# Buffers shifted to multiples of 128 bytes, the first norm's squares added on VectorE, and a mixer projection that waits for emptied banks and has a third pair of weight tiles

## The reference

```python
def hybrid_layer(x, ...):                        # first layer, T = 512, D = 1024
    h = rmsnorm(x, g_mix)                        # x * rsqrt(mean(x*x)) * g
    z = h @ w_in                                 # 7 parts of 1024 features
    rnn_x, rnn_y, conv_b, conv_c, conv_x, gate_rnn, gate_conv = split(z)
    rnn_x = causal_depthwise_conv(rnn_x, conv4_w) + conv4_b
    y_rnn = gelu(rnn_y) * rg_lru(rnn_x, ..., lru_lambda)   # 4 heads; a scan over the tokens
    y_conv = conv_b * causal_depthwise_conv(conv_c * conv_x, conv3_w)
    merged = sigmoid(gate_rnn) * y_rnn + sigmoid(gate_conv) * y_conv
    x = x + merged @ w_out                       # the mixer projection
    g, u = split(rmsnorm(x, g_ffn) @ w_gate_up)
    x = x + (silu(g) * u) @ w_down               # 2816 wide
    return x + sigmoid(rmsnorm(x, g_ple) @ w_ple_gate) * (p @ w_ple)
# second layer: projections, sparse and latent attention, an output projection, then
#   a layer of 16384 experts: every token's product with all expert rows u (gelu),
#   top 16 of 8 heads chosen by product keys, weighted sum of the expert rows v
```

## The kernel before

| Tile | Role | Bytes past a multiple of 128 |
|---|---|---|
| `spl` | stationary | 64 |
| `w3` | stationary | 96 |
| `hh`, `hl`, `hu`, `lu`, `mixh`, `mixl`, `wsp` | moving | 96 |
| `acth`, `actl` | moving | 32 |

## Time and profile before

### The profile page before, as it was taken

One profiled execution on the slowest core, in us unless ns is written; L12 is line 12 of the kernel. 1 busy time (PEld: TensorE's weight loads), 2 busy tenths in 40 slices (PEclk: granted clock), 3 DMA queues, 4 the chain that ended last, 5 costly groups with the idle time before them and its releaser, 6 DMA issues.

```text
span 2835.9 us, 37050 instructions
## 1 busy us (share of the span) xinstructions
PE 2731.8 (96%) x13240; PEld 2244.3 (79%) x13240; DVE 1830.4 (65%) x2459; ACT 907.9 (32%) x1531; POOL 1691.3 (60%) x755
## 2 busy tenths in 40 slices
PE   7999989999998999998999999999999999999999
PEld 6777768878775776445888888888898999999998
DVE  5999963262225434665539983999963677777776
ACT  2223212101122234664234443444432333333332
POOL 5888867777764621002745455777776565665564
PEclk9999989999998998999999999999999999999999
DMA  3343324323322322001334546888898666766664
GB/s 141 132 133 129 126 101 137 129 95 130 121 93 72 104 81 103 1 1 47 117 106 139 146 143 181 258 279 282 282 319 310 231 259 238 265 244 254 256 241 159
DMA packets 171119, 466.66 MB, mean 165 GB/s; under 512 B 12832, under 2 KB 86688, under 8 KB 171040
## 3 DMA queue, kind: packets, MB, share of 16 engines
q1 hardware_dynamic: 152608, 398.53, 42.1%
q0 software_dynamic: 18432, 67.12, 6.6%
HBM read 404.78 MB, written 60.82 MB: 164 GB/s over the span
## 4 chain that ended last, share of the span: by engine, by line
PE 83%; issue 7%; DVE 4%; POOL 4%; ACT 1%; DMA 0%; POOLq 0%; SPq 0%; DVEq 0%; ACTq 0%
PE ps L1013 37%; PE ps L547 32%; POOL spl L2074 3%; PE ps L948 2%; PE ps L1034 2%; PE ps L925 1%; PE ps L908 1%; PE ps L641 1%; PE ps L563 1%; PE ps L904 1%; PE ps L569 1%; PE ps L867 1%; PE ps L736 1%; PE ps L701 0%; PE ps L813 0%
## 5 line engine op out<-in xcount | busy, mean ns | idle before, releaser
L2074 POOL TENSOR_TENSOR spl<-ring,spl 128x1024 fp32r<-128x1024 f32 x256 | 660.4, 2580 | 513.7 <-ACT spl L1367 513.6
L2016 POOL TENSOR_TENSOR spl<-ring,zero 128x1024 fp32r<-128x1024 f32 (+2 forms) x181 | 365.4, 2019 | 561.5 <-PE ps L547 499.6
L547 PE MATMUL ps<-hh,spl 128*128 128x512 f32 x2064 | 664.8, 401 | 17.7 <-DVE hl L1493 7.3
L1013 PE MATMUL ps<-wsp,spl 128*128 128x448 f32 x3072 | 638.6, 370 | 4.6 <-issue 4.6
L1013 PEld LDWEIGHTS ps<-wsp,spl 128*128 128x128 f32 x3072 | 578.7, 189 | 62.2 <-POOL spl L2074 5.0
L1013 PE MATMUL ps<-hh,spl 128*128 128x448 f32 x2048 | 606.6, 372 | 5.8 <-POOL spl L2074 5.8
L1367 ACT ACTIVATE spl<-ring 128x1024 fp32r<-128x1024 f32 x256 | 271.7, 1061 | 817.2 <-PE ps L1013 815.5
L2018 POOL TENSOR_TENSOR spl<-ring,spl 128x1024 fp32r<-128x1024 f32 (+2 forms) x181 | 481.3, 2659 | 14.2
L547 PEld LDWEIGHTS ps<-hh,spl 128*128 128x128 f32 x2064 | 391.0, 189 | 124.5 <-issue 14.0
L1974 DVE TENSOR_TENSOR wsp<-gl,wsp 128x448 fp32r<-128x448 f32 x128 | 310.6, 2427 | 184.1 <-ACT wsp L1412 183.9
L1013 PEld LDWEIGHTS ps<-hh,spl 128*128 128x128 f32 x2048 | 385.2, 188 | 46.5 <-issue 8.6
(11 more groups left out here) (338 smaller groups left out, 3348.2 us busy)
## 6 DMA issues: line engine op xcount, KB each, us to landing
ring<-stream_in SPq DMA_DIRECT2D x196, 704.0 KB, 4.1
ring<-u_in SPq DMA_DIRECT2D x128, 512.0 KB, 4.1
ring<-v_in SPq DMA_DIRECT2D x128, 512.0 KB, 3.5
gelu<-gst SPq DMA_DIRECT2D x128, 224.0 KB, 4.2
dense<-stage SPq DMA_DIRECT2D x14, 2048.0 KB, 13.5
gl<-gelu SPq DMA_DIRECT2D x32, 896.0 KB, 5.8
gw<-dense SPq DMA_DIRECT2D x32, 896.0 KB, 8.5
x<-x_in SPq DMA_DIRECT2D x4, 512.0 KB, 6.2
```

The source lines that it names most:

```text
L547: m = pe.matmul(ps[:, bank, :], w[:, part, k0 + k * n:k0 + k * n + P], rhs(k), start=first and k == 0 and part == 0 and rhs is high, stop= ...
L1013: m = pe.matmul(ps[:, bank, 0:TD], w[:, part, k0 + k * P:k0 + (k + 1) * P], rhs(k), start=first and k == 0 and part == 0 and rhs is high, ...
L2016: pool.tensor_tensor(w[:, 0, 0:n], ring[:, j, 0:n], zero[:, :].to_broadcast([P, n]), ALU.add).then_inc(wt_high, 1)
L2074: pool.tensor_tensor(spl[:, j % 2, 1, 0:D], ring[:, j, 0:D], spl[:, j % 2, 0, 0:D].bitcast(F32), ALU.subtract).then_inc(lo_done, 1)
```

## The change

1. Pads (`lead`, `mid`, `gap`) and another order of the buffers put every operand named in the table above at a multiple of 128 bytes, `w3` and the new `w4` too, and with them most other operands of matmuls (`identb`, `mqk`, `qk`, `xc`, `hnt`, `blk`, `pr`, `pt`). `cst`, with the ones and the identity, stays 64 bytes past one.
2. The first norm is done like the others: ACT squares chunk 0 into PSUM bank 7 and the rest into `sq1`, DVE adds them (7 additions), PE sums the result once (4 matmuls, 8 instructions). DVE does this and the scaling of the norm ahead of most of the softplus steps, which now stand behind them; ACT waits for them (`sp_ready`) at the first tanh.
3. The units 0 to 3 of the mixer projection wait until ACT has emptied their bank (`z_evac`) in place of `x_add`. The third unit has a tile pair of its own, `w4`, which lies where head 3 had `xc` and `r_g`; POOL splits it when the seventh chunk is merged (`chunk_done`), whatever PE has finished.

```diff
@@ buffers
+        rn = sb("rn", [P, 2, TT])
+        sb("lead", [P, 8])
...
-        rn = sb("rn", [P, 2, TT])
...
+        sp = sb("sp", [P, 6, DC], c=mix)
         mix.close()
...
-        sp = sb("sp", [P, 6, DC], c=one)
         rg = ExitStack()
-        rxp = sb("rxp", [P, 2, 3 + T], c=rg)
-        prod = sb("prod", [P, 2, 2 + T], c=rg)
+        mixh = [sb("mixh0", [P, DC // 2, T], F32R, c=rg), mixh1]
         zb = {n: sb(f"z_{n}", [P, 2, T], c=rg) for n in ("ry", "cb", "cc", "cx", "gr", "gc")}
+        fourth = ExitStack()
+        w4 = sb("w4", [P, 2, D], F32R, c=fourth)
+        fourth.close()
...
+        rxp = sb("rxp", [P, 2, 3 + T], c=rg)
+        prod = sb("prod", [P, 2, 2 + T], c=rg)
+        sb("mid", [P, 16], c=rg)
...
-        mixh = [mixh1, sb("mixh0", [P, DC // 2, T], F32R, c=rg)][::-1]
...
+        sb("gap", [P, 24], c=two)
@@ PE
             def mixed(c, k0, k1, ready=None):
                 if k0 == 0:
-                    pe.wait_ge(x_add, X_BASE[U_OUT] + c + 1)
+                    if c < 4:
+                        pe.wait_ge(z_evac, HEADS_RG * 14 + c + 4)
+                    else:
+                        pe.wait_ge(x_add, X_BASE[U_OUT] + c + 1)
                     pe.wait_ge(wt_low, U_OUT + c + 1)
-                return split_products(3 + c % 4, spl[:, c % 2, :, :], ...
+                return split_products(3 + c % 4, w4[:, :, :] if c == 2 else spl[:, c % 2, :, :], ...
...
-            for c in range(DC):
-                pe.wait_ge(col_sq, c + 1)
-                column(sq1[:, c % SQ_RING, :], c == 0, c == DC - 1)
+            added_column(0)
             row(0)
@@ ACT
-                if c >= SQ_RING:
-                    eng.wait_ge(col_used, c - SQ_RING + 1)
-                eng.activation(sq1[:, c % SQ_RING, :], x[:, c, :], ACT.Square).then_inc(col_sq, 1)
+                square_of(0, c)
...
-            eng.wait_ge(sp_ready, 2)
...
+                        if first:
+                            eng.wait_ge(sp_ready, 2)
@@ DVE
+            dve.sem_inc(x_add, 4)
...
+            for c in range(1, DC):
+                add_square(0, c)
+            column_inverse(0)
+            scale_parts(0, "g_mix")
             dve.wait_ge(sp_exp, 1)
...
-            column_inverse(0)
-            scale_parts(0, "g_mix")
...
-            dve.sem_inc(x_add, 4)
             for k in range(DC - 2, DC):
                 mix_part(k, k + 1)
@@ POOL
-                    pool.wait_ge(col_used, DC)
+                    pool.wait_ge(col_used, 1)
...
-            with pool.Fori(1, U_DOWN // RING) as i:
+            with pool.Fori(1, U_OUT // RING) as i:
+                for j in range(RING):
+                    group(i, j)
+            single(U_OUT)
+            single(U_OUT + 1)
+            pool.wait_ge(w_ready[2], 16 * (U_OUT // RING + 1))
+            pool.wait_ge(chunk_done, 2 + DC - 1)
+            unit_parts(2, U_OUT + 3, w=w4[:, :, :])
+            single(U_OUT + 3)
+            with pool.Fori(U_OUT // RING + 1, U_DOWN // RING) as i:
```

More of the change, by code:

```diff
@@ L564, in norm, with added_column @@
                 m.then_inc(ss_ready, 1)
-            def column(rows, first=True, last=True):
+            def added_column(n):
+                pe.wait_ge(col_add, (COLUMNS.index(n) + 1) * (DC - 1))
+                rows = (sq7 if n == 7 else sq1)[:, SQ_RING, :]
                 for t in range(TT):
-                    m = pe.matmul(ps[:, 7, t:t + 1], rows[:, t * P:(t + 1) * P], ones[:, 0:1],
-                                  start=first and t == 0, stop=last and t == TT - 1)
+                    m = pe.matmul(ps[:, 7, t:t + 1], rows[:, t * P:(t + 1) * P], ones[:, 0:1], start=True, stop=True)
                 m.then_inc(col_used, 1)
-            def added_column(n):
-                pe.wait_ge(col_add, COLUMNS.index(n) * (DC - 1))
-                column((sq7 if n == 7 else sq1)[:, SQ_RING, :])
             def row(n):
@@ L596, in mixed @@
                 if k0 == 0:
-                    pe.wait_ge(x_add, X_BASE[U_OUT] + c + 1)
+                    if c < 4:
+                        pe.wait_ge(z_evac, HEADS_RG * 14 + c + 4)
+                    else:
+                        pe.wait_ge(x_add, X_BASE[U_OUT] + c + 1)
                     pe.wait_ge(wt_low, U_OUT + c + 1)
-                return split_products(3 + c % 4, spl[:, c % 2, :, :], k0 * P, k1 - k0, P, lambda k: mixh[(k0 + k) // 4][:, (k0 + k) % 4, :],
+                return split_products(3 + c % 4, w4[:, :, :] if c == 2 else spl[:, c % 2, :, :], k0 * P, k1 - k0, P, lambda k: mixh[(k0 + k) // 4][:, (k0 + k) % 4, :],
                                       lambda k: mixl[:, k0 + k, :], k0 == 0, k1 == DC, ready)
@@ L1104, in square_of @@
             def square_of(n, c):
-                at = (COLUMNS.index(n) - 1) * (DC - 1)
+                at = COLUMNS.index(n) * (DC - 1)
                 if c > SQ_RING:
@@ L1114, in column_root @@
                 at = COLUMNS.index(n)
-                eng.wait_ge(col_used, DC + at)
+                eng.wait_ge(col_used, at + 1)
                 eng.activation(rn[:, 0, :], ps[:, 7, 0:TT], ACT.Sqrt, scale=1.0 / D, bias=pc("eps")).then_inc(col_root, 1)
@@ L1500, in column_inverse @@
                 dve.reciprocal(rn[:, 0, :], rn[:, 0, :]).then_inc(col_inverse, 1)
+            def add_square(n, c):
+                rows = sq7 if n == 7 else sq1
+                dve.wait_ge(col_sq, COLUMNS.index(n) * DC + c + 1)
+                if c > 1:
+                    dve.wait_ge(col_add, COLUMNS.index(n) * (DC - 1) + c - 1)
+                dve.tensor_tensor(ps[:, 7, :] if c < DC - 1 else rows[:, SQ_RING, :], ps[:, 7, :],
+                                  rows[:, (c - 1) % SQ_RING, :], ALU.add).then_inc(col_add, 1)
             def raw_part(n, c, g, high, low):
@@ L1507, in raw_part @@
                 if c:
-                    rows = sq7 if n == 7 else sq1
-                    dve.wait_ge(col_sq, COLUMNS.index(n) * DC + c + 1)
-                    if c > 1:
-                        dve.wait_ge(col_add, (COLUMNS.index(n) - 1) * (DC - 1) + c - 1)
-                    dve.tensor_tensor(ps[:, 7, :] if c < DC - 1 else rows[:, SQ_RING, :], ps[:, 7, :],
-                                      rows[:, (c - 1) % SQ_RING, :], ALU.add).then_inc(col_add, 1)
+                    add_square(n, c)
+            dve.sem_inc(x_add, 4)
             def fma(dst, a, w, b):
```

## The result

| | Before | After |
|---|---|---|
| Median (four runs each) | 2835.9 us | 2787.7 us (2780.0 to 2792.8) |
| Ratio, 95% interval | | 0.9825 (0.9804 to 0.9846) |
| Profiled execution: time, span | 2838.0, 2835.9 us | 2788.3, 2786.5 us |
| PE busy | 2731.8 us (96%) | 2673.9 us (96%), 13184 matmuls |
| DVE, POOL busy | 1830.4, 1691.3 us | 1865.4, 1708.2 us |

Faster, as predicted, but by 1.7% and not by 6%; the time lies above the range of 2640 to 2752. With 2780 to 2793 the runs also lie further apart than the first ones of before.

What follows compares the result with a forecast made beforehand. PE's matmuls bound the kernel. Gains of 46 + 22 + 20 + 53.8 + 10.6 + 6.1 + 13 = 171.5 us from the profiled 2838.0 give 2666.5, so 2664 us at the median; range 2640 to 2752.

Steps and rivals of the forecast that it cites:

- What bounds the kernel: Whole kernel: PE, at 96% of the span, makes it as long as its matmuls, so the cost of one decides.
- Part 1: Split-product matmuls in heads, projection and expert layer: operands at multiples of 128 bytes save 17.5 ns on each of 10300.
- The block: Row reads in SBUF: an unaligned row tile touches one more 128-byte block, 13.3 ns per matmul; block only had chance 0.17.
- the earlier trace: Rows at 1.2 GHz and in plain float32 without excess, read as fitting a reader that pays per block touched.
- the other 6.7 ns: Matmuls with `spl`, not `w3`: weight load and row stream in each other's way, 233.3 against 226.7 ns.
- the pace of `w3` for all: Rival for all split-product matmuls: only 6.7 ns gained, from how both operands stand to each other; 2750 us, chance 0.09.
- The last 128 units: End of the expert layer: 3072 matmuls at 17.5 ns less, 53.8 us, nothing else near as a bound.
- The heads: Heads follow DVE, whose wait for PE's `z_cx` goes: 10.6 us gained.
- Part 2: First norm: scaling 6.5 us earlier, softplus steps hidden in DVE's wait for the first convolution; 6.1 us gained.
- Part 3: Mixer projection: third unit 4.5 us after the last `merged` in place of 17.7; 13 us gained.
- DMA and POOL as followers: Rival: POOL, DVE or DMA keep 20 to 40 us of the gain; 2684 to 2704 us, chance 0.10.

Runs made afterwards that it cites:

- part 1 alone: Kernel before with only the new pads and order of the buffers: 2800.8 us, 0.9867 of the kernel before.
- experiments 1, 3, 7: Kernels of matmuls alone, without the computation: 16 pairs of tile starts; row distances in 32-byte steps; 8-byte steps and other widths. At 512 columns 226.7 ns at best.
- Experiment 4: Changed kernel with 128 bytes between `spl` and rows: 2803.9 us; with everything moved 32 bytes: 2783.3; again unchanged: 2782.1.
- the first trace of after: Profiled execution of the changed kernel in the main measurement: 2788.3 us.
- the second trace: Trace of the changed kernel measured again, unchanged: 6.2 us shorter than its first trace; median of that measurement 2782.1 us.
- experiment 6: Changed kernel with 13 softplus steps ahead of the additions, memsets and release ahead of the scaling: 2795.6 us; with `spl` also moved in the expert layer: 2765.1.
- experiment 1: Matmuls alone, without the computation: 16 pairs of tile starts, other widths and fewer weight columns; equal pairs took 233.2 to 233.4 ns at 512 columns.

## Why the prediction was wrong

**What bounds the kernel** was right: PE kept 96% and the pace of its matmuls decided: part 1 alone brought 36 us.

**Part 1, the step that failed**, in the prediction's words: "the block goes, `w3` shows that the rest can go with it". The block does not exist. In place of 17.5 ns, a matmul of 512 columns became 6.6 ns shorter (233.3 to 226.7) and one of 448 columns 4.0 (206.7 to 202.7). At 448 and 512 columns at least 13.3 ns over the columns are there at every distance and every start tried, aligned or not (experiments 1, 3, 7), and of the three types in fp32r alone. I had taken a number that fitted (32 columns are 128 bytes, 17 blocks for 16) for a mechanism. No row of before could tell it from a fixed cost of the type: the earlier trace rows, which I read as support, fit that as well, since they differ in clock and in type. What the 13.3 ns are stays open. The weights' columns, the change of weights, the partitions and the neighbours are ruled out.

**What was left is the other 6.7 ns**, and there the rival "the pace of `w3` for all", with the condition "if the gain lies in how both operands stand to each other and not in the blocks", named the mechanism. It had 0.09. Experiment 4 shows this in both directions. Its price of 85 us was too high (49 in the traces) for three reasons. At 448 columns distance 0 gives 4.0 and not 6.7 ns, and that only in one of its two states. In the first part of the expert layer the mean pace fell by 2 ns, from 206.0 to 204.0, since only part of the units there got the better one; where they did, PE's pause after every fourth unit grew, from 0.54 to 0.63 us from start to start. And waits took their share: for the 512 columns the rival's 18 us came out with part 1 alone (18.6), but in the changed kernel PE waits 2.7 us for DVE at 1371 us (0.6 before) and then runs at the lower clock level for a while, 3.2 us in all. Another 2.8 us went between 857 and 888 us in the first trace of after, not in the second; no run shows why.

**The two rules against which it was held.** The Trainium skill's SBUF, State Buffer, under Specifications (TRN2), has cachelines of 16 bytes; by that rule the prediction said the shift would be worth nothing. Here distances that are all multiples of 16 have different paces (226.7 ns at 0, 233.4 at 32, 229.1 at 64), and they come again after 256 bytes, so a rule of 16-byte lines does not give it. The Trainium skill's TensorE: Matmul & The Clock Gate, under "Step-by-step: what each phase is for", says that loading the next weights takes no SBUF bandwidth from the running matmul, over a read port of its own. The traces speak against it for fp32r: where the weights stand against the rows changes the pace by up to 13 ns; that the two reads disturb each other is argued from this, not shown. The N / 2.4 + 2.5 ns of the same page of the Trainium skill fits bf16 (215.8, 189.2 ns), but not fp32r (226.7 and 200.0 at best).

**The last 128 units** (53.8 predicted, 11.9 measured). The gain is not that of the alignment. With distance 0, traces had 202.7 or 206.7 ns there, 12 us apart, and with the old distance 32 they had 204.4 or 206.7. Before happened to stand at the slow end, after at the fast end: that was luck. With both at the slow end the gain is 0.5 us, as part 1 alone shows, and with both at the fast end 1.7 ns x 3072, 5 us. The first part of the expert layer shows more of these states. There PE pauses after every fourth unit, and between two pauses the pace, once settled, is mostly one and the same: 204.4 or 206.7 ns before, 202.7 or 206.7 after. In after the units from 1484.7 us have 202.7, those from 1504.7 have 206.7, those from 1547.3 have 202.7 again, all with the same addresses. So the state changes over a pause, within one execution; what chooses it is open. It can be part of the spread of the runs (before's went from 2814 to 2841), but not all of it. At distance 64 no trace shows a second state, and the runs lie 3 to 7 us apart.

**The heads** (10.6 predicted): right that they follow DVE and that the wait for `z_cx` goes. Part 1 alone brought 6.1 of the 8.4 us that 1248 matmuls at 6.7 ns are worth. With part 2 in front, PE gains 1.6 over them; the second trace, without the fall of the clock at 61 us, has 4.9.

**Part 2** (6.1 predicted, 4.3 to 4.7 up to the first matmul): the first addition came at 10.65 and not 9.9, mainly since ACT began the squares 0.6 us later (9.41 in place of 8.77), and the step of `hl` ahead of the first matmul took 1.73 us (0.89 before). The wrong step is "now they run where DVE waited 5.13 us for the first convolution, so they cost at most some tenths": I named DVE's wait as the cover, but what DVE waited for, ACT's copy, itself waits for a release that stands behind the steps. Without that cover I had priced them at 5.1; they took 10.4, because three of them lasted as long as a split of POOL beside them. They pushed ACT's copy from 36.2 us, where experiment 6 has it, to 44.9, and PE's lead fell from 5.4 us at the 96th matmul to 1.7 at the 192nd. Experiment 6 says what this was worth: 1.3 us at the end of the heads.

**Part 3** (13 predicted, 11.0 measured): right, third unit included (4.5 predicted, 5.1 and 3.6 measured in the two traces).

**DMA and POOL as followers**: not seen. In the last 100 us of the middle part the DMA share is 0.92, and it still gained, and with distance 64 it gave 3 to 4 us more. Whether they would have capped the paces that I forecast, no run shows.

## What to carry to other kernels

When an excess over the columns fits a nice number of bytes, measure matmuls by themselves with the address as the only thing changed, before a sum is made of it: one such kernel of a millisecond would have replaced my 17.5 ns. In a kernel of split fp32r products, choose the distance between weights and rows for each width: here 0 modulo 256 for 512 columns, 64 for 448. And before a step is moved behind another, follow what its engine releases there, not only what the engine itself waits for.

## What was not expected of the hardware

- The pace of fp32r matmuls that follow each other depends on the distance of both addresses modulo 256: at 512 columns 226.7 ns (0), 229.1 (64), 232 to 235 (21 of the 32 steps of 8 bytes, all other multiples of 32 among them), 239.9 (120).
- At 448 columns some distances have two stable paces (202.7 and 206.7 ns at 0; 204.4 and 206.7 at 32). A stretch of 3072 matmuls without a pause stays in one to the end; over a pause it can change.
- Five DVE steps of 0.17 us, in the two traces of after, began behind the start of a split of POOL, and each lasted until POOL's instruction had ended, up to 2.26 us.
- fp32r with 128 columns took 214.2 ns a matmul and with 256 columns 119.0 (experiment 1, distance 128).
- After 2.5 us without a matmul PE went for 3.7 us at the lower clock level in one execution (granted clock 0.86 in 5 us) and not in another of the same program.
